# A 64-wide recurrence on Trainium2: its loads cut into 512 KB pieces along the inverse levels, its output products moved between the last three levels

## The chip, the cores and the metric

The kernel runs on one core of one Trainium2 chip. The metric is device time of one execution in microseconds (us); the median over three runs of the kernel before is 5277.31 us (5276.41 to 5279.03). A core has five engines with instruction streams of their own: PE (TensorE, matrix products), DVE (VectorE), ACT (ScalarE), POOL (GpSimd) and SP (SyncE, which here only issues transfers). They meet through semaphores; 16 DMA engines move data between HBM and the on-chip memory.

## What is computed

The reference is a model of two mixing blocks and one block with attention. The change touches one part of the first mixer, a recurrence over 1024 time steps, 8 heads of width 64, run once forward and once backward in time:

```python
def rwkv7_scan(r, w, k, v, a, b):
    def step(state, xs):
        r_t, w_t, k_t, v_t, a_t, b_t = xs
        sa = jnp.einsum('bhvk,bhk->bhv', state, a_t)
        state = state * w_t[:, :, None, :] + sa[..., None] * b_t[:, :, None, :] + v_t[..., None] * k_t[:, :, None, :]
        return state, jnp.einsum('bhvk,bhk->bhv', state, r_t)
    _, y = lax.scan(step, jnp.zeros((bsz, heads, hd, hd), jnp.float32), xs)
...
    wkv = rwkv7_scan(r, w_f, k, v, a_vec, b_vec) + flip_t(
        rwkv7_scan(flip_t(r), flip_t(w_b), flip_t(k), flip_t(v), flip_t(a_vec), flip_t(b_vec)))
```

The kernel does not step through time. It takes chunks of 64 steps: within a chunk the dependence of the steps on each other is a triangular 64 x 64 system, whose inverse is built by doubling, and only the state goes from chunk to chunk.

## The kernel before

The kernel is one long program of stages. The stage of the change is the function `rwkv` (L2041 on), from about 838 us to 1386 us of the profiled execution. Before it an earlier stage writes the decayed factors to HBM (`decayed`, six arrays per direction, and `shared`, of which array 2 holds the values); after it `mixer_outputs` reads the result `yk` and 14 tiles that `rwkv` has prefetched into the buffer `early`.

All of it is done for two directions d = 0 and d = 1, for 16 chunks (RCH) of 64 steps (RH), and for 4 pairs of heads (RPAIRS): a tile [128, 4, 64] holds the 8 heads, two on the partitions (64 each) and four along the free dimension. `by_head` (L2087) issues the products of one term: for each pair h and each half e one 64 x 64 x 64 product in f32, 8 products, which the trace records as 16 matmuls of 64 x 64. That block of 16 records is the unit in which PE's work is counted here. A call with several terms adds them in the same PSUM region.

The loop of PE (L2204 on) has RCH + 1 = 17 turns. Turn i has an inner half, the inverse of chunk i, and an outer half, the state and the outputs of chunk k = i - 1. The order on PE is written out by hand:

- `begin` of both directions (5 blocks each): products of the loaded factors into bank Y, and transposes of values and keys into banks A and D; `gates` (2 blocks each) into bank G.
- level 0 of the inverse: `level_y` (1 block); with it `read_state` (2 blocks) of the chunk before.
- level 1: `level_y`, then `solve` (1 block), then `level_z` (2 blocks).
- level 2: for each direction `level_y` and behind it `outputs` of the chunk before (5 blocks: two state terms, three y terms); then `level_z`.
- levels 3, 4 and 5: `level_y` of both directions, `level_z` of both (2 blocks each, 1 at level 5, where only xt is wanted).

Turn 0 has no outer half, turn 16 no inner one. At each level l >= 1 a chain goes round the engines: Y on PE (needs x of the level before), its copy `ys` on ACT (L2264), Z on PE (the products D and A from ys and xt), then DVE adds D to x (L2331) and A to xt (L2333). Each engine runs its list in order, direction 0 before direction 1.

Further in the outer half: ACT copies `rest` and `u` (L2257, L2270); DVE makes the new state from the first half of bank G (L2340), in its list at level 2 behind the two directions' additions; ACT copies the output y from the second half of bank G to `yk` (L2274), in its list at level 3, and waits for y_out (the products are done) and s_ready (the state is made).

Loads: a group is four chunks (GROUP = 4), 7 arrays of [512, 256] f32 per direction, 512 KB each. Two buffers per direction alternate (`given`; the first lies in `early`). SP issues per group and direction one transfer of 3072 KB (six arrays) and one of 512 KB (L2110, L2111). Groups 0 and 1 are issued at the start, group q >= 2 for direction d when the outputs of all chunks of group q - 2 are done (y_out at 4(q - 1)). PE's `begin` waits for both transfers of its group. When the outputs of chunk 11 are done, SP issues the 14 prefetch transfers of 512 KB for the next stage (L2120). POOL makes the masked blocks `off` of levels 1 to 5 (L2129).

Of the kernel before, what the change touches and what calls it, by code (L numbers as in the profile page):

```python
# [27 lines left out]
P = 128  # L28
# [1506 lines left out]
RPAIRS = 4  # L1535
RCH = T // RH
# [504 lines left out]
def rwkv(nc, tag, decayed, shared, last_decay, consts, early, yk, early_in, prefetch):  # L2041
# [16 lines left out]
    with Stage(nc, tag) as st:  # L2058
# [25 lines left out]
        def pairs(t):  # L2084
            return t.unsqueeze(1).to_broadcast([P, RPAIRS, RH])

        def by_head(pe, out, *terms):  # L2087

            for h in range(RPAIRS):
                for n, (a, b) in enumerate(terms):  # L2090
                    for e in range(2):
                        own = slice(RH * e, RH * e + RH)
                        mm = pe.matmul(out[own, h, :], a[own, h, :], b[own, h, :], start=(n == 0), stop=(n == len(terms) - 1))  # L2093
            return mm

        with nc.Block(no_gpsimd_drain=True) as block:
            @block.sync
            def _(sp):
                for a, b in ((ident[:, :], consts["ident64"]), (masks[:, :, :, :], consts["masks64"]),
                             (strict[:, :, :], consts["strict_half"]), (incl[:, :, :], consts["incl64"])):  # L2100
                    sp.dma_start(a, b).then_inc(const_in, 16)

                def load(q):
                    for d in range(2):
                        if q >= 2:
                            sp.wait_ge(per[d]["y_out"], GROUP * (q - 1))
                        at = GT * (q if d == 0 else RCH // GROUP - 1 - q)
                        split = lambda x: x.rearrange("n (k p) t -> p (n k) t", p=P)[:, :, at:at + GT]
                        to = given[d][q % 2].rearrange("p n k t -> p (n k) t")
                        sp.dma_start(to[:, 0:24, :], split(decayed[d])).then_inc(per[d][f"in{q % 2}"], 16)  # L2110
                        sp.dma_start(to[:, 24:28, :], split(shared[2:3])).then_inc(per[d][f"in{q % 2}"], 16)  # L2111

                load(0)
                load(1)
                for q in range(2, RCH // GROUP):
                    load(q)
                for d in range(2):
                    sp.wait_ge(per[d]["y_out"], RCH - GROUP)
                for slot, source in prefetch:
                    sp.dma_start(early[:, slot, :], source).then_inc(early_in, 16)  # L2120

            @block.gpsimd
# [12 lines left out]
            def _(pe):  # L2135
# [4 lines left out]
                def begin(d, i):  # L2140
                    s = per[d]
                    A, Y, DD, G = banks[d]
                    pe.wait_ge(s[f"in{i // GROUP % 2}"], 32 * (i // GROUP // 2 + 1))
                    pe.wait_ge(s["x_ready"], i * XN)
                    by_head(pe, Y[:, first, :], (piece(d, i, 1), piece(d, i, 0)))
                    by_head(pe, Y[:, second, :], (piece(d, i, 2), piece(d, i, 0))).then_inc(s["aa"], 1)
                    by_head(pe, A[:, first, :], (piece(d, i, 6), one))
                    by_head(pe, A[:, second, :], (piece(d, i, 3), one)).then_inc(s["vb_turned"], 1)
                    by_head(pe, DD[:, first, :], (piece(d, i, 4), one)).then_inc(s["k_turned"], 1)
# [29 lines left out]
                def read_state(d, k):  # L2179
                    s, b, t = per[d], bufs[d], turns[d][k % 2]  # L2180
                    G = banks[d][3]
                    pe.wait_ge(s["s_ready"], k)
                    pe.wait_ge(s["vb_copied"], k + 1)
                    pe.wait_ge(s["g_ready"], min(k + 2, RCH))
                    by_head(pe, G[:, first, :], (piece(d, k, 0), b["s"]), (t["aa"][:, second, :], t["vb"][:, first, :])
                            ).then_inc(s["read"], 1)
# [5 lines left out]
                    pe.wait_ge(s["x_ready"], (k + 1) * XN)  # L2192
                    by_head(pe, G[:, second, :], (t["xt"], b["rest"])).then_inc(s["u_done"], 1)

                def outputs(d, k):
                    s, b, t = per[d], bufs[d], turns[d][k % 2]
                    G, gk = banks[d][3], g[d][k % 2]
                    pe.wait_ge(s["u_copied"], k + 1)
                    by_head(pe, G[:, first, :], (t["vb"][:, second, :], b["u"]), (t["kt"], t["vb"][:, first, :]))
                    by_head(pe, G[:, second, :], (b["s"], piece(d, k, 5)), (b["u"], gk[:, first, :]),  # L2200
                            (t["vb"][:, first, :], gk[:, second, :])).then_inc(s["y_out"], 1)

                for i in range(RCH + 1):
                    inner, outer = i < RCH, i > 0  # L2204
                    for d in range(2):
                        if inner:
                            begin(d, i)
                    for d in range(2):
                        if inner:
                            gates(d, i)  # L2210
                    for d in range(2):
                        if inner:
                            level_y(d, i, 0)
                        if outer:
                            read_state(d, i - 1)
                    for d in range(2):
                        if inner:
                            level_y(d, i, 1)
                    for d in range(2):
                        if outer:  # L2220
                            solve(d, i - 1)
                        if inner:
                            level_z(d, i, 1)
                    for d in range(2):
                        if inner:
                            level_y(d, i, 2)
                        if outer:
                            outputs(d, i - 1)
                    if inner:
                        for d in range(2):  # L2230
                            level_z(d, i, 2)
                        for l in range(3, LV):
                            for d in range(2):
                                level_y(d, i, l)
                            for d in range(2):
                                level_z(d, i, l)

            @block.scalar
            def _(act):
                for i in range(RCH + 1):  # L2240
# [17 lines left out]
                    for l in range(1, LV):  # L2258
# [6 lines left out]
                        for d in range(2):  # L2265
                            s = per[d]
                            if outer and l == 1:
                                act.wait_ge(s["u_done"], k + 1)
                                act.wait_ge(s["y_out"], k)
                                act.activation(bufs[d]["u"][:, :, :], banks[d][3][:, second, :], ACT.Copy).then_inc(s["u_copied"], 1)  # L2270
                            if outer and l == 3:
                                act.wait_ge(s["y_out"], k + 1)
                                act.wait_ge(s["s_ready"], k + 1)
                                act.activation(yk[:, d, :, chunk(d, k) * RH:(chunk(d, k) + 1) * RH], banks[d][3][:, second, :],  # L2274
                                               ACT.Copy).then_inc(s["y_copied"], 1)

            @block.vector
            def _(dve):
# [5 lines left out]
                for i in range(RCH + 1):  # L2284
# [38 lines left out]
                    for l in range(1, LV):  # L2323
# [10 lines left out]
                                                  ALU.add).then_inc(s["x_ready"], 1)  # L2334
                        for d in range(2):
                            s, b = per[d], bufs[d]
                            if outer and l == 2:
                                dve.wait_ge(s["s_decayed"], k + 1)
                                dve.wait_ge(s["y_out"], k + 1)
                                dve.tensor_tensor(b["s"][:, :, :], b["sd"][:, :, :], banks[d][3][:, first, :],  # L2340
# [3366 lines left out]
```

## Time and profile before

| | |
|---|---|
| median of the runs | 5277.31 us |
| profiled execution, its span | 5269.1 us |
| PE busy | 4796.6 us, 91% of the span |
| DVE, ACT, POOL busy | 2724.4, 1100.7, 731.5 us |
| the stage, from its first DMA issue to the last copy of y | 838.3 to 1386.1 us |
| of it PE on the products of Y and Z | banky 107.0, banka 109.0, bankd 87.6 us |

The profile is of one execution; the span runs from the first to the last instruction, and the measured time of a run includes what lies around it. Lines name an engine, a source line and an operation with output and inputs; since `by_head` issues all products, they all stand on L2093 and are told apart by their tiles: `rk_banky<-rk_x,rk_off` is Y, `rk_bankd<-rk_ys,rk_xt` and `rk_banka<-rk_xt,rk_ys` are the two products of Z, `rk_bankg<-...` belongs to gates, state and outputs, and the first products of a turn are `rk_banky<-kept_held` or `rk_banky<-rk_in`, after the two load buffers. PEclk is the mean granted clock of PE, 1.00 being 2.4 GHz. A releaser "issue" means that the engine waited for nothing that the profile shows. Turn i begins at 854.22 (i = 0), 894.21, 924.62, 955.83, 986.41, 1021.56, 1057.14, 1087.54, 1117.95, 1154.08, 1188.18, 1218.70, 1249.11, 1281.99, 1316.25, 1346.87 and 1377.19 us; direction 1 of turn 0 starts at 865.66 us, when its data is there. SP issues the loads of group 2 from 1002.5, of group 3 from 1134.9 and the prefetch from 1268.1 us.

### The profile page before, as it was taken

The numbers are of one execution on the slowest core, as the hardware profiler recorded it, in microseconds if no ns is written. First come the engines' busy times: TensorE is split into PE (matmuls) and PEld (weight loads), VectorE is DVE, ScalarE is ACT, GpSimd is POOL, SyncE is SP. The second block draws the span as 40 slices with busy tenths as digits, with TensorE's granted clock in tenths as the row PEclk, the third lists the DMA queues.
The fourth block names the chain that finished last, engine by engine and source line by source line (L and its number), as shares of the span: only waits on it lengthen the run. The fifth ranks groups of instructions, "written<-read, shape, count | busy, mean of one in ns | idle before, by whom it ended". The sixth has DMA issues, their size and how long they took to land. (4 is left out here: it accounts for less than half of the span.)

```text
span 5269.1 us, 88450 instructions
## 1 busy us (share of the span) xinstructions
PE 4796.6 (91%) x38282; PEld 3690.1 (70%) x38282; DVE 2724.4 (52%) x3644; ACT 1100.7 (21%) x1513; POOL 731.5 (14%) x666
## 2 busy tenths in 40 slices
PE   9996997999889999888849999999988989999999
PEld 7775987999768767544437767766544557788887
DVE  5776543444445788467765594232563325443342
ACT  2443221222313232101102221111221122110010
POOL 0001331111000164000000010012000000241340
PEclk9998998999898999989979899999999999999999
DMA  4444114111121334512222153246212014212113
GB/s 141 147 161 138 47 41 126 60 60 60 44 92 60 111 140 170 199 64 85 98 82 100 57 166 101 75 115 167 46 25 52 5 43 151 76 48 91 70 50 99
DMA packets 223077, 482.78 MB, mean 92 GB/s; under 512 B 34599, under 2 KB 101097, under 8 KB 222181
## 3 DMA queue, kind: packets, MB, share of 16 engines
q1 hardware_dynamic: 177428, 342.80, 20.1%
q0 software_dynamic: 33392, 117.54, 6.5%
q10 hardware_dynamic: 11872, 16.78, 0.9%
q8 instruction: 306, 5.01, 0.4%
q14 instruction: 79, 0.64, 0.0%
HBM read 332.21 MB, written 142.35 MB: 90 GB/s over the span
## 5 line engine op out<-in xcount | busy, mean ns | idle before, releaser
L4966 PE MATMUL tail_product<-tail_x_hi,tail_w_hi 128*128 128x512 f32 x832 | 329.4, 396 | 12.9 <-DVE tail_x_lo L165 10.9
L4966 PE MATMUL tail_product<-tail_x_lo,tail_w_hi 128*128 128x512 f32 x832 | 325.1, 391 | 0.0
L4966 PE MATMUL tail_product<-tail_x_hi,tail_w_lo 128*128 128x512 f32 x832 | 324.4, 390 | 0.0
L3653 PE MATMUL win_product<-kept_hn_hi,win_w_hi 128*128 128x512 f32 x560 | 230.3, 411 | 8.7 <-DVE kept_hn_lo L3807 6.3
L1777 PE MATMUL front_product<-kept_x_hi,front_w_hi 128*128 128x512 f32 x544 | 220.9, 406 | 10.7 <-DVE kept_x_lo L165 10.5
L3653 PE MATMUL win_product<-kept_hn_lo,win_w_hi 128*128 128x512 f32 x560 | 221.0, 395 | 0.0
L3653 PE MATMUL win_product<-kept_hn_hi,win_w_lo 128*128 128x512 f32 x560 | 220.7, 394 | 0.0
L1777 PE MATMUL front_product<-kept_x_hi,front_w_lo 128*128 128x512 f32 x544 | 213.8, 393 | 0.0
L1777 PE MATMUL front_product<-kept_x_lo,front_w_hi 128*128 128x512 f32 x544 | 213.3, 392 | 0.0
L2770 PE MATMUL oproj_product<-kept_mix_hi,oproj_w_hi 128*128 128x512 f32 x512 | 205.3, 401 | 8.6 <-DVE kept_mix_lo L165 8.6
L2770 PE MATMUL oproj_product<-kept_mix_hi,oproj_w_lo 128*128 128x512 f32 x512 | 200.4, 391 | 0.0
L2770 PE MATMUL oproj_product<-kept_mix_lo,oproj_w_hi 128*128 128x512 f32 x512 | 200.2, 391 | 0.0
L4966 PE MATMUL tail_product<-tail_f_hi,tail_w_hi 128*128 128x512 f32 x480 | 189.6, 395 | 0.0
L4966 PEld LDWEIGHTS tail_product<-tail_x_hi,tail_w_hi 128*128 128x128 f32 x832 | 156.8, 188 | 45.5 <-issue 11.5
L4966 PE MATMUL tail_product<-tail_f_hi,tail_w_lo 128*128 128x512 f32 x480 | 186.8, 389 | 0.0
L4966 PE MATMUL tail_product<-tail_f_lo,tail_w_hi 128*128 128x512 f32 x480 | 186.7, 389 | 0.0
L4966 PEld LDWEIGHTS tail_product<-tail_x_hi,tail_w_lo 128*128 128x128 f32 x832 | 156.8, 188 | 33.0
L4966 PEld LDWEIGHTS tail_product<-tail_x_lo,tail_w_hi 128*128 128x128 f32 x832 | 157.0, 189 | 31.0 <-issue 0.2
L3288 PE MATMUL lc_ps<-lc_idft,lc_zz 128*128 128x256 f32 x512 | 120.6, 400 | 61.9 <-DVE lc_zz L3131 59.2
L3288 PEld LDWEIGHTS lc_ps<-lc_idft,lc_zz 128*128 128x128 f32 x512 | 102.7, 202 | 81.6 <-issue 62.4
L2129 POOL TENSOR_TENSOR rk_off<-rk_aa,rk_masks 128x1280 f32<-128x1280 f32 x32 | 99.2, 3115 | 428.7 <-DVE rk_aa L2293 428.7
L2331 DVE TENSOR_TENSOR rk_x<-rk_x,rk_bankd 128x256 f32<-128x256 f32 x128 | 53.9, 421 | 200.4 <-PE rk_banka L2093 200.4
(748 smaller groups left out, 11271.2 us busy)
## 6 DMA issues: line engine op xcount, KB each, us to landing
s_decayed<-front_ring SPq DMA_DIRECT2D x96, 256.0 KB, 3.9
tail_w<-in_w_gu SPq DMA_DIRECT2D x44, 512.0 KB, 3.2
second_raw<-in_w_in SPq DMA_DIRECT2D x35, 512.0 KB, 3.6
front_w<-in_even_w SPq DMA_DIRECT2D x34, 512.0 KB, 3.9
s_pm<-kept_held SPq DMA_DIRECT2D x64, 256.0 KB, 2.0
win_cq_hi_plain<-in_ada_w POOLq DMA_DIRECT2D x16, 1024.0 KB, 5.4
oproj_ring<-in_odd_w POOLq DMA_DIRECT2D x30, 512.0 KB, 3.8
dn_kv<-s_qkv SPq DMA_DIRECT2D x16, 768.0 KB, 6.7
```

The source lines that it names most:

```text
L1777: mm = pe.matmul(pp[:, u_, f, :], p, q, start=(k == 0 and m == 0), stop=(k == 7 and m == 2))
L2129: pool.tensor_tensor(off[d][:, 1:, :, :], turns[d][i % 2]["aa"][:, first, :].unsqueeze(1).to_broadcast([P, LV - 1, RPAIRS, RH]), masks[:, ...
L2331: dve.tensor_tensor(b["x"][:, :, :], b["x"][:, :, :], DD[:, first, :], ALU.add).then_inc(s["x_ready"], 1)
L2770: mm = pe.matmul(pp[:, u, f, :], p, q, start=(k == 0 and m == 0), stop=(k == 7 and m == 2))
L3288: mm = pe.matmul(out[:, 2 * s + r // 2, r % 2 * 256:r % 2 * 256 + 256], zz[:, r, kind, f, ct * P:(ct + 1) * P], tabi[:, kind, f, r, :], st ...
L3653: mm = pe.matmul(pp[:, u, h, :], l, b, start=(k == 0 and m == 0), stop=(k == depth(s) - 1 and m == 2))
L4966: mm = pe.matmul(pp[:, s % 2, h_, :], l, b, start=(k == 0 and m == 0), stop=(k == deep(s) - 1 and m == 2))
```

## The change

It has two parts. First, SP loads every array by itself, 512 KB each: 14 transfers per group. Group 0 is issued at once. For groups 1, 2 and 3 each transfer waits for one more Y of direction 0 (y_done counts six per turn): the first for Y of level 3 in the first turn of the group before, the 14th for 13 Y's later; directions alternate. The wait for the outputs that still read the buffer stays. The 14 prefetch transfers are spaced in the same way from turn 12, level 3. PE's `begin` waits for seven transfers (112) instead of two (32).

Second, `outputs` is divided. `state_terms` (the two terms that make the new state) stays between the Y's of level 2. The three terms of y go, pair by pair of heads, ahead of the Y's of levels 3, 4 and 5: pairs 0 to 2 of direction 0, then pair 3 of direction 0 with pairs 0 and 1 of direction 1, then pairs 2 and 3 of direction 1. DVE's addition that completes the state and ACT's copy of y are put at level 4 for direction 0 and at level 5 for direction 1, both behind that level's work. `read_state` waits in addition for ACT's copy of the y before.

```diff
@@ by_head
-        def by_head(pe, out, *terms):
+        def by_head(pe, out, *terms, heads=range(RPAIRS)):
-            for h in range(RPAIRS):
+            for h in heads:
@@ SP
-                def load(q):
-                    for d in range(2):
-                        if q >= 2:
-                            sp.wait_ge(per[d]["y_out"], GROUP * (q - 1))
...
-                        sp.dma_start(to[:, 0:24, :], split(decayed[d])).then_inc(per[d][f"in{q % 2}"], 16)
-                        sp.dma_start(to[:, 24:28, :], split(shared[2:3])).then_inc(per[d][f"in{q % 2}"], 16)
+                def piece_in(q, d, n):
+                    at = GT * (q if d == 0 else RCH // GROUP - 1 - q)
+                    source = decayed[d][n] if n < 6 else shared[2]
+                    sp.dma_start(given[d][q % 2][:, n, :, :], tiled(source)[:, :, at:at + GT]).then_inc(per[d][f"in{q % 2}"], 16)
+                def paced(first_level, j):
+                    sp.wait_ge(per[0]["y_done"], first_level + j)
+                for d in range(2):
+                    for n in range(7):
+                        piece_in(0, d, n)
+                for q in range(1, RCH // GROUP):
+                    begun = GROUP * (q - 1) * LV
+                    for n in range(7):
+                        for d in range(2):
+                            if q >= 2 and n == 0:
+                                sp.wait_ge(per[d]["y_out"], GROUP * (q - 1))
+                            paced(begun + 4, 2 * n + d)
+                            piece_in(q, d, n)
                 for d in range(2):
                     sp.wait_ge(per[d]["y_out"], RCH - GROUP)
-                for slot, source in prefetch:
+                for j, (slot, source) in enumerate(prefetch):
+                    paced((RCH - GROUP) * LV + 4, j)
@@ PE
+                    pe.wait_ge(s["y_copied"], k)
...
+                def state_terms(d, k):
+                    pe.wait_ge(s["u_copied"], k + 1)
+                    by_head(pe, banks[d][3][:, first, :], (t["vb"][:, second, :], b["u"]), (t["kt"], t["vb"][:, first, :]))
+                def outputs(d, k, heads):
+                    mm = by_head(pe, banks[d][3][:, second, :], (b["s"], piece(d, k, 5)), (b["u"], gk[:, first, :]),
+                                 (t["vb"][:, first, :], gk[:, second, :]), heads=heads)
+                    if heads[-1] == RPAIRS - 1:
+                        mm.then_inc(s["y_out"], 1)
+                FILL = {3: [(0, range(0, 3))], 4: [(0, range(3, 4)), (1, range(0, 2))], 5: [(1, range(2, 4))]}
@@ PE, the loop
-                            outputs(d, i - 1)
+                            state_terms(d, i - 1)
...
-                        for l in range(3, LV):
+                    for l in range(3, LV):
+                        if outer:
+                            for d, heads in FILL[l]:
+                                outputs(d, i - 1, heads)
+                        if inner:
@@ ACT, the copy of y
-                            if outer and l == 3:
+                            if outer and l == 4 + d:
@@ DVE, the new state
-                            if outer and l == 2:
+                            if outer and l == 4 + d:
```

## Rows read from the trace of the kernel before

**Rows 1.** The head of the page.

```profile
span 5269.1 us, 88450 instructions
```

**Rows 2.** Windows by turn: us, then busy us of each engine, PEclk, DMA share, GB/s.

```profile
865.66:894.21 28.55, 23.45 (x625) 21.86 (x625) 10.35 (x26) 4.81 (x12) 3.14 (x1) 0.92 0.73 232
...
986.41:1021.56 35.15, 32.21 (x964) 31.38 (x961) 14.21 (x32) 7.66 (x20) 6.18 (x2) 0.90 0.56 179
1021.56:1057.14 35.58, 31.42 (x965) 30.47 (x961) 13.21 (x32) 7.74 (x20) 6.25 (x2) 0.95 0.12 36
1057.14:1087.54 30.40, 29.63 (x964) 28.82 (x961) 14.23 (x32) 7.66 (x20) 6.19 (x2) 1.00 0.01 4
...
1117.95:1154.08 36.13, 31.92 (x965) 30.64 (x961) 14.16 (x32) 7.67 (x20) 6.18 (x2) 0.95 0.55 176
1154.08:1188.18 34.10, 31.44 (x964) 30.49 (x961) 13.21 (x32) 7.77 (x20) 6.28 (x2) 0.95 0.12 37
...
1249.11:1281.99 32.88, 30.45 (x964) 29.67 (x961) 14.21 (x32) 7.66 (x20) 6.18 (x2) 0.97 0.41 157
1281.99:1316.25 34.26, 31.02 (x964) 29.93 (x962) 13.21 (x32) 7.66 (x20) 6.26 (x2) 0.98 0.19 72
```

**Rows 3.** Timeline of PE in one turn: start us, us, engine, line, tiles, count.

```profile
1061.82 2.06 PE L2093 MATMUL rk_bankg<-rk_in 64*64 64x64 f32 x64
1063.69 0.66 PE L2093 MATMUL rk_banky<-rk_ident,rk_off 64*64 64x64 f32 x16
...
1077.22 0.66 PE L2093 MATMUL rk_banka<-rk_xt,rk_ys 64*64 64x64 f32 x16
1077.89 0.68 PE L2093 MATMUL rk_banky<-rk_x,rk_off 64*64 64x64 f32 x16
1078.82 0.68 PE L2093 MATMUL rk_banky<-rk_x,rk_off 64*64 64x64 f32 x16 [0.25 <-DVE rk_xt L2333]
1079.31 0.66 PE L2093 MATMUL rk_bankd<-rk_ys,rk_xt 64*64 64x64 f32 x16
...
1086.27 1.35 PE L2093 MATMUL rk_banka<-rk_xt,rk_ys 64*64 64x64 f32 x32
```

**Rows 4.** Timeline of DVE in the same turn, level 2.

```profile
1078.59 0.74 DVE L2340 TENSOR_TENSOR rk_s<-rk_sd,rk_bankg 128x256 f32<-128x256 f32 x2
```

**Rows 5.** Timeline of ACT in the same turn, level 3.

```profile
1078.61 0.39 ACT L2264 ACTIVATE rk_ys<-rk_banky 128x256 f32<-128x256 f32 x1 [4.50 <-PE rk_banky L2093]
1079.54 0.38 ACT L2264 ACTIVATE rk_ys<-rk_banky 128x256 f32<-128x256 f32 x1 [0.55 <-PE rk_banky L2093]
1079.82 0.66 ACT L2274 ACTIVATE kept_held<-rk_bankg 128x256 f32<-128x256 f32 x2
```

**Rows 6.** Timeline of all engines in the last turn, where two handovers are bare.

```profile
1379.27 0.38 ACT L2257 ACTIVATE rk_rest<-rk_bankg 128x256 f32<-128x256 f32 x1 [0.55 <-PE rk_bankg L2093]
1379.71 0.55 PEld L2093 LDWEIGHTS rk_bankg<-rk_rest,rk_xt 64*64 64x64 f32 x16 [0.15 <-ACT rk_rest L2257]
...
1382.84 0.42 DVE L2340 TENSOR_TENSOR rk_s<-rk_sd,rk_bankg 128x256 f32<-128x256 f32 x1 [4.34 <-PE rk_bankg L2093]
...
1383.36 0.38 ACT L2274 ACTIVATE kept_held<-rk_bankg 128x256 f32<-128x256 f32 x1 [2.54 <-DVE rk_s L2340]
```

**Rows 7.** Timeline of PE while the loads of group 2 run.

```profile
1011.24 0.48 PE L2093 MATMUL rk_bankd<-rk_ys,rk_xt 64*64 64x64 f32 x5 [2.15 <-issue]
...
1026.36 0.85 PE L2093 MATMUL rk_banka<-rk_ident,rk_in 64*64 64x64 f32 x22 [3.39 <-issue]
```

**Rows 8.** DMA queues in 1002.5 to 1026.5 (two rows), then in 1057.14 to 1087.54.

```profile
q1 hardware_dynamic: 7232, 7.34, 95.3%
q8 instruction: 3, 0.05, 0.9%
...
q8 instruction: 7, 0.11, 1.4%
```

**Rows 9.** Who waited for whom, PE, 865.66 to 894.21: us in total, times, longest.

```profile
PE rk_banka L2093 <- issue: 2.2, 1, 2.2
```

More of the change, by code:

```diff
@@ L2101, in _ @@
                     sp.dma_start(a, b).then_inc(const_in, 16)
-                def load(q):
-                    for d in range(2):
-                        if q >= 2:
-                            sp.wait_ge(per[d]["y_out"], GROUP * (q - 1))
-                        at = GT * (q if d == 0 else RCH // GROUP - 1 - q)
-                        split = lambda x: x.rearrange("n (k p) t -> p (n k) t", p=P)[:, :, at:at + GT]
-                        to = given[d][q % 2].rearrange("p n k t -> p (n k) t")
-                        sp.dma_start(to[:, 0:24, :], split(decayed[d])).then_inc(per[d][f"in{q % 2}"], 16)
-                        sp.dma_start(to[:, 24:28, :], split(shared[2:3])).then_inc(per[d][f"in{q % 2}"], 16)
[L2113 to L2116, printed above, removed]
+                def piece_in(q, d, n):
[15 more added lines that the diff above has]
+                            piece_in(q, d, n)
                 for d in range(2):
                     sp.wait_ge(per[d]["y_out"], RCH - GROUP)
-                for slot, source in prefetch:
+                for j, (slot, source) in enumerate(prefetch):
+                    paced((RCH - GROUP) * LV + 4, j)
                     sp.dma_start(early[:, slot, :], source).then_inc(early_in, 16)
@@ L2142, in begin @@
                     A, Y, DD, G = banks[d]
-                    pe.wait_ge(s[f"in{i // GROUP % 2}"], 32 * (i // GROUP // 2 + 1))
+                    pe.wait_ge(s[f"in{i // GROUP % 2}"], 112 * (i // GROUP // 2 + 1))
                     pe.wait_ge(s["x_ready"], i * XN)
@@ L2193, in solve @@
                     by_head(pe, G[:, second, :], (t["xt"], b["rest"])).then_inc(s["u_done"], 1)
-                def outputs(d, k):
+                def state_terms(d, k):
                     s, b, t = per[d], bufs[d], turns[d][k % 2]
-                    G, gk = banks[d][3], g[d][k % 2]
                     pe.wait_ge(s["u_copied"], k + 1)
-                    by_head(pe, G[:, first, :], (t["vb"][:, second, :], b["u"]), (t["kt"], t["vb"][:, first, :]))
-                    by_head(pe, G[:, second, :], (b["s"], piece(d, k, 5)), (b["u"], gk[:, first, :]),
-                            (t["vb"][:, first, :], gk[:, second, :])).then_inc(s["y_out"], 1)
+                    by_head(pe, banks[d][3][:, first, :], (t["vb"][:, second, :], b["u"]), (t["kt"], t["vb"][:, first, :]))
+                def outputs(d, k, heads):
+                    s, b, t = per[d], bufs[d], turns[d][k % 2]
+                    gk = g[d][k % 2]
+                    mm = by_head(pe, banks[d][3][:, second, :], (b["s"], piece(d, k, 5)), (b["u"], gk[:, first, :]),
[3 more added lines that the diff above has]
+                FILL = {3: [(0, range(0, 3))], 4: [(0, range(3, 4)), (1, range(0, 2))], 5: [(1, range(2, 4))]}
                 for i in range(RCH + 1):
```

## The prediction

> **What bounds the kernel now.** I read the page's span first, then busy time and granted clock by iteration of the stage that the change touches, then the timelines of PE, DVE and ACT inside one iteration, and last the DMA traffic where iterations are long. The profiled execution spans 5269.1 us [rows 1]; the runs shown have a median of 5277.3, 8.2 above it, and I carry that offset along. Only the recurrence changes (from about 838 to 1386 us, 17 turns of a loop). There PE is the engine with work all the time: in an undisturbed turn, 1057.14 to 1087.54, it is busy 29.63 of 30.40 us at full clock, DVE 14.2, ACT 7.7, POOL 6.2 [rows 2]. A turn with products and inverse both is 60 blocks of 16 matmul records (one term for one direction). Four such blocks take 1063.69-1061.82 = 1.87 us, 0.467 each [rows 3], so the work alone is 28.0 us. The other 2.4 us are four holes, at the start of levels 3, 4 and 5 and of the next turn. I call T0 the start of the last block of a level (product A of direction 1). At T0 = 1077.22 the block runs to +0.47; Y of direction 0 starts at +0.67, Y of direction 1 at +1.60, Z of direction 0 at +2.09 [rows 3]. Three blocks are 1.40, so the hole is 0.69. Its end is set by DVE, which adds the last update to x and xt of direction 1 before Y of direction 1 may start. The fourth hole: the 32 records from 1086.27 need 0.93, the next turn starts at 1087.54, 1.27 later: 0.34 [rows 2, 3].
>
> Six turns are longer than 30.40: 35.15, 35.58, 36.13, 34.10, 32.88 and 34.26, together 208.1, which is 25.7 above six undisturbed ones [rows 2]. In all of them DMA moves data, at a mean of 36 to 179 GB/s against 4, and the mean granted clock is 0.90 to 0.98 [rows 2]. Inside, PE stands still for 2.15 and 3.39 us with "issue" as releaser, so no semaphore kept it [rows 7]. Instructions come by DMA too: queue q8 moved 7 packets in the undisturbed 30.4 us, one in 4.3 us (0.11 MB, so 16 KB each), but only 3 in the 24 us in which q1 moved 7.34 MB at 95% of the engines [rows 8]. I read the stalls as instruction blocks that came late behind load packets; each is followed by a stretch at the lower of the two clocks (1.2 instead of 2.4 GHz), which the mean clock shows.
>
> **Part 1: the loads.** Before, a group of four chunks loads 7.34 MB in one burst of some 24 us; after, it is 14 pieces of 512 KB, one behind each Y of direction 0 from level 3 of the first turn of the group before. At q1's 7.34 MB in 24 us, 306 GB/s [rows 8], a piece is under way for 1.7 us, and levels 3 to 5 are 3.5 us apart. In flight time is 14 x 1.7 = 24 us, as before, but spread over 14/6 = 2.3 turns, 69 us. What goes: the 25.7 us of the six turns, and the 2.2 us stall in turn 0, which overlaps the burst for group 1 [rows 9]; 27.9 us. What comes back: about 16 instruction blocks are fetched in 69 us, 24/69 of them, 5.6, beside a piece. Each may wait between nothing and one whole piece, 1.7 us; four spread loads (three groups and the prefetch for the next stage, which is 14 transfers too) bound this from 0 to 4 x 5.6 x 1.7 = 38 us. I take 1 us per load, 4 us, near the lower end: the mean rest of a piece is 0.85, an engine's share is 32 packets, and PE has always some instructions in hand (the undisturbed turns show no stall with "issue" at all although every block is fetched just in time). A stall of under 1 us should not cost clock: DVE-caused holes of that size stand in every undisturbed turn at clock 1.00 [rows 2]. Part 1: 27.9 - 4 = 23.9 us.
>
> The Trainium skill (DMA: Bandwidth & Descriptors, section Queues, rings and completion order) says that a DMA engine goes round its queues packet by packet, and that a packet is at most 64 descriptors. By that rule a fetch waits for one packet whatever the size of the transfer, and cutting the transfers gains nothing; the sum would be Part 2 alone. The stalls of 2.15 and 3.39 us speak of long waits but don't decide between "a fixed number of descriptors" and "all that is queued".
>
> **The first load** is the same 7.34 MB in the same order (direction 0, then 1), in 14 issues instead of 4. The bytes set its length, not the count of issues: cost 0. Pieces of the later groups come in time: the 14th is released 13 Y's after the first, in turn 2 of 4, a turn and a half before its use. The waits that SP adds stand before nothing but SP's own loads. The prefetch is released from turn 12, level 3, until turn 14, 2 turns before the stage ends.
>
> **Part 2: the output products.** Before, all five terms of the outputs stand between Y of level 2 of the two directions. After, the two state terms (2 blocks, 0.93 us) stay there and the three y terms (3 blocks, 1.40 us per direction, 0.35 per head pair) go ahead of levels 3, 4, 5: 3, 3 and 2 pairs, so 1.05, 1.05 and 0.70 us. Level 2 still has cover: Y of direction 1 needs +1.60 from its T0, as above [rows 3], and gets 0.47+0.47+0.93 = 1.87 at least. In levels 3 and 4 the fill moves Y of direction 1 to +0.47+1.05+0.47 = 1.99, beyond 1.60: DVE is hidden. What is late next is ACT: it starts to copy y 0.72 after Y of direction 0 began (1077.89 to 1078.61 [rows 3, 5]), takes 0.38, PE's weight load follows 0.06 later (1379.27+0.38 to 1379.71 [rows 6]) and the matmul about 0.05 behind it: Z can start 1.21 after Y, and PE has 0.93 of work. A hole of 0.28 stays; 0.69-0.28 = 0.41 gained, twice.
>
> Level 5 gains less. The copy of y moves to the same level as the state's add (level 4 for direction 0), and ACT waits there for the add. DVE comes to it 1.37 after T0 (1078.59-1077.22 [rows 3, 4]), takes 0.42, ACT follows 0.10 later (1382.84 to 1383.36 [rows 6]): +1.89. Queued behind it on ACT is y of direction 0, level 5, ready at 0.47+0.70+0.72 = +1.89; the spacing of two copies is 0.28 (1079.54 to 1079.82 [rows 5]), so it starts at +2.17 and Z at +2.66, where PE would be free at +2.10. Hole 0.56, gain 0.13. Direction 1's pair falls into level 5: DVE's add then ends about 0.9 after the next turn begins, its next work comes 1.2 after; covered by 0.3, and if not, that is the price. The added wait of PE, y copied before the state is read, has everything of PE behind it, but that copy ends some 4 us before; cost 0. The fourth hole stays. Sum: 0.41+0.41+0.13 = 0.95 per turn, 15 turns with both halves: 14.2 us. Turn 0 has no products and the last turn nothing but products in the same order: 0. Bounds: from 0 (each fill only moves the hole) to 15 x 3 x 0.69 = 31.
>
> **Sum.** 23.9+14.2 = 38.1 us. The profiled execution would be 5231.0, the median 5277.3-38.1 = 5239.
>
> **Rivals.**
> (a) Fetches wait for a fixed number of packets, so the same stall time is only strewn about: gain 14.2, 5263. For it: the skill's rule above. Against: the bursts queue 448 KB per engine, a piece 32 KB, less than what the measured stalls need.
> (b) The holes move and don't close, the loads gain: 5277.3-23.9 = 5253. For it: the chain Y, ACT, Z, DVE per level is not shortened, only overlapped; against: the numbers above leave PE 1.05 us to fill 0.69.
> (c) Nothing of a fetch's wait shows, and ACT's chain overlaps more than I think: 27.9+28 = 56, 5221.
> (d) Slower: in a burst a late block holds PE back, so only two fetches per load are hit; strewn pieces may hit 5.6 fetches per load, each with a stall of 2.4 and the loss of clock behind it. One such event now costs 25.7/6 = 4.3 us; 4 x 5.6 x 4.3 = 96 us against 27.9+14.2 gained: 5277.3+54 = 5331. It decides from 42/22.4 = 1.9 us per hit on, more than a piece is under way.
> (e) It doesn't act as described (the paced loads land late, or the stalls have another cause and the fill is nothing): 5277.
>
> **Numbers.** Forecast 0.60 (its own range 5230 to 5250); (a) 0.14, (b) 0.11, (c) 0.07, (d) 0.04, (e) 0.04. The range takes in (a), (b) and part of (c): 5226 to 5265. A measurement of this kernel tells some 0.2%, 10.6 us, from no change. Faster 0.90 (the forecast, (b), (c) and most of (a)), same 0.05, slower 0.05.
>
> **What would show it.** Step 1: turns 4 to 7 of the loop within 1 us of each other, clock 1.00 throughout after 871 us, "issue" stalls of PE under 1 us. Step 2: undisturbed turns of 29.4 to 29.6 us; at levels 3 and 4 PE waits for ACT's ys instead of DVE's xt, for 0.2 to 0.3; at level 5 ACT's copy of y stands right ahead of ys. The prediction is wrong if stalls over 1.5 us with "issue" remain (a, d) or if undisturbed turns stay over 30 us (b).

## The result and the profile after

The changed kernel takes 5236.36 us (median of 4 runs, 5233.85 to 5239.42) against 5276.86 for the kernel before (4 runs, 5272.28 to 5279.03): ratio 0.9932, 95% interval 0.992 to 0.9944. A second comparison gave 5246.3 against 5272.4, ratio 0.9947 (0.9926 to 0.9968). The forecast was 5239 in 5226 to 5265.

The profiled execution spans 5232.0 us, 37.1 less than before [rows 1]. The stage itself, from its first DMA issue to its last copy of y, went from 547.8 to 515.8 us, by 32.0; the other 5.1 us lie in stages that the change doesn't touch. In the profiles of this study all that lies outside the stage takes between 4713 and 4738 us without an edit there, so I count the 32.0 and leave the 5.1 to chance. Another execution of the changed kernel has 519.0 us in the stage.

Windows by turn, as in [rows 2]; the first window is the first load, the second turn 0 from direction 1 on (its first product starts at 865.33):

```profile
838.30:854.86 16.56, 0.00 (x0) 0.03 (x1) 0.18 (x1) 0.00 (x0) 0.00 (x0) 0.50 0.97 305
865.10:889.13 24.03, 22.15 (x625) 20.92 (x625) 10.27 (x25) 4.72 (x12) 3.14 (x1) 0.93 0.18 56
889.13:921.17 32.04, 29.78 (x964) 28.80 (x961) 12.99 (x32) 7.40 (x19) 6.27 (x2) 1.00 0.32 103
...
1011.35:1041.15 29.80, 29.07 (x960) 28.45 (x961) 14.23 (x33) 7.68 (x20) 6.18 (x2) 1.00 0.39 122
1041.15:1071.98 30.83, 29.31 (x960) 28.51 (x961) 14.23 (x33) 7.67 (x20) 6.18 (x2) 1.00 0.31 99
1071.98:1101.32 29.34, 28.86 (x961) 28.35 (x961) 14.21 (x33) 7.67 (x20) 6.17 (x2) 1.00 0.02 5
...
1192.54:1223.73 31.19, 29.84 (x961) 28.76 (x961) 13.32 (x33) 7.68 (x20) 6.27 (x2) 1.00 0.02 4
...
1253.19:1285.08 31.89, 29.51 (x960) 28.64 (x961) 13.34 (x33) 7.68 (x20) 6.17 (x2) 1.00 0.38 132
```

An undisturbed turn takes 29.33 us instead of 30.40. The granted clock is 1.00 in every turn after turn 0, where six turns had 0.90 to 0.98. Turns with loads are not clean, though: up to 2.7 us above 29.33, and one without any load traffic (1192.54, 4 GB/s) is 1.9 above it. Such turns stood in the kernel before too (924.62: 31.21 us at 4 GB/s, 0.8 above 30.40).

PE in the undisturbed turn, from the last block of level 2 on, to be laid beside [rows 3] (blocks of the products in between are left out):

```profile
1089.27 0.66 PE L2093 MATMUL rk_banka<-rk_xt,rk_ys 64*64 64x64 f32 x16
1090.79 1.13 PE L2093 MATMUL rk_banky<-rk_x,rk_off 64*64 64x64 f32 x32
1091.92 0.68 PE L2093 MATMUL rk_bankd<-rk_ys,rk_xt 64*64 64x64 f32 x16
...
1097.45 0.63 PE L2093 MATMUL rk_banka<-rk_xt,rk_ys 64*64 64x64 f32 x16
1098.62 1.10 PE L2093 MATMUL rk_banky<-rk_x,rk_off 64*64 64x64 f32 x32
1100.02 1.15 PE L2093 MATMUL rk_banka<-rk_xt,rk_ys 64*64 64x64 f32 x32 [0.30 <-ACT rk_ys L2284]
```

Both Y's now run as one block of 32 records: the wait for DVE between them is gone. Level 3: T0 to Y 1.52, Y to Z 1.13. Level 5: Y to Z 1.40, and here ACT is the releaser. DVE and ACT around that hole:

```profile
1098.80 0.41 DVE L2360 TENSOR_TENSOR rk_s<-rk_sd,rk_bankg 128x256 f32<-128x256 f32 x1
...
1099.31 0.38 ACT L2294 ACTIVATE kept_held<-rk_bankg 128x256 f32<-128x256 f32 x1 [2.89 <-DVE rk_s L2360]
1099.59 0.65 ACT L2284 ACTIVATE rk_ys<-rk_banky 128x256 f32<-128x256 f32 x2
```

ACT was idle for 2.89 us, waited for the new state, copied y, and only then came to ys. Who kept PE waiting from 870 to 1354 us (us in total, times, longest):

```profile
PE rk_banka L2093 <- ACT rk_ys L2284: 4.5, 15, 0.3
PE rk_banky L2093 <- issue: 3.9, 6, 1.5
PE rk_bankd L2093 <- issue: 1.7, 4, 0.9
PE rk_bankg L2093 <- issue: 1.5, 3, 0.8
PE rk_banka L2093 <- issue: 1.0, 2, 0.7
PE rk_banky L2093 <- DVE rk_xt L2353: 1.0, 4, 0.3
```

"issue" sums to 8.1 us, none over 1.5 (18.7 before, up to 3.4); DVE's xt fell from 12.0 to 1.0. Of the 8.1, 7.7 lie in turns 1 to 15; the other 0.4 is in the last turn and is a wait of another kind (shown further down).

The ledger of the stage, in us gained: turns 1 to 15 took 483.0 and take 454.9. Of these 28.1, 15 x (30.40 - 29.33) = 16.0 are the shorter undisturbed turn, and 12.1 are what lay above it (27.0 before, 14.9 after). Turn 0 with its wait for direction 1 went from 40.0 to 34.3: 5.7. The first load took 1.1 longer, the last turn 0.65. Together 32.0. The first load and turn 0 belong together: PE starts direction 1 when its data is there, 27.3 us after the stage's start before and 27.5 after. So the 1.1 us delays direction 0 alone and is won back in the wait for direction 1; from direction 1's start, turn 0 is 4.75 us shorter. In it PE had stalls with "issue" of 2.2, 0.9 and 0.2 us before and none after, and it is busy for 22.15 us instead of 23.45.

### The profile page after: what moved, and what is told of

The parts are those of the page before. It is cut to its first block and busy times, and to the rows that moved or that the text cites. A ratio compares the mean times of both kernels' runs of the same rounds, so it can differ in the third digit from the quotient of the medians.

```text
span 5232.0 us, 88526 instructions
## 1 busy us (share of the span) xinstructions
PE 4770.3 (91%) x38282; PEld 3668.8 (70%) x38282; DVE 2724.5 (52%) x3644; ACT 1101.0 (21%) x1513; POOL 732.9 (14%) x666
## 5 line engine op out<-in xcount | busy, mean ns | idle before, releaser
L4986 PE MATMUL tail_product<-tail_x_hi,tail_w_hi 128*128 128x512 f32 x832 | 329.4, 396 | 11.9 <-DVE tail_x_lo L165 10.8
L3673 PEld LDWEIGHTS win_product<-kept_hn_hi,win_w_hi 128*128 128x128 f32 x560 | 106.4, 190 | 60.7 <-issue 32.1
```

The costliest lines, as they stand in the source:

```text
L3673: mm = pe.matmul(pp[:, u, h, :], l, b, start=(k == 0 and m == 0), stop=(k == depth(s) - 1 and m == 2))
L4986: mm = pe.matmul(pp[:, s % 2, h_, :], l, b, start=(k == 0 and m == 0), stop=(k == deep(s) - 1 and m == 2))
```

## The experiments

One number is used throughout: the loss, turns 1 to 15 together less 15 undisturbed turns (of 30.40 us in the old order of products, 29.33 in the new one). It holds what late instructions cost. The stalls are those of the whole stage from 870 us on, turn 0 included. Stage, loss and stalls are of one profiled execution each.

| kernel | stage us | loss us | PE stalls with "issue" us | median us (before, same chip) |
|---|---|---|---|---|
| before | 547.8 | 27.0 | 18.7 | |
| loads alone | 538.9 | 21.8 | 12.7 | 5267.4 (5274.1) |
| loads alone, again | 538.3 | 20.1 | 10.8 | 5262.9 (5270.2) |
| products alone | 535.0 | 28.9 | 23.8 | 5266.0 (5274.1) |
| changed | 515.8 | 14.9 | 8.1 | 5236.4 (5276.9) |
| changed, again | 519.0 | 17.1 | 11.5 | 5246.3 (5272.4) |
| pieces not paced | 537.3 | 30.8 | 24.7 | 5251.6 (5272.4) |
| pieces in pairs | 524.7 | 22.6 | 16.7 | 5246.2 (5272.4) |
| pieces one Z later | 519.7 | 19.3 | 10.0 | 5247.4 (5272.9) |
| halves | 514.4 | 13.3 | 7.7 | 5238.9 (5272.9) |
| no loads of groups 2 and 3, group 1 at the start | 512.4 | 6.7 | 5.1 | 5237.5 (5272.4) |
| both copies at level 5 | 520.7 | 19.4 | 13.3 | 5243.4 (5274.1) |
| split fill | 516.3 | 26 (from 28.6) | 15.8 | 5238.3 (5274.1) |
| split fill, halves | 507.6 | 17 (from 28.6) | 9.6 | 5233.5 (5272.9) |

**Each part alone.** The kernel before with the SP block and the 112 of the change (e1), and the changed kernel with SP's block of before (e2).

```diff
e1_loads, on the kernel before
-                for q in range(2, RCH // GROUP):
-                    load(q)
+                            paced(begun + 4, 2 * n + d)
+                            piece_in(q, d, n)
...
e2_products, on the changed kernel
-                            paced(begun + 4, 2 * n + d)
-                            piece_in(q, d, n)
+                for q in range(2, RCH // GROUP):
+                    load(q)
```

> Only the loads are changed (14 paced pieces per group); the output products stay as before. Theory A (part 1 is worth what the changed kernel's trace shows, turn 0 and the long turns, 16 us in the stage, and the rest of the gain lies in other stages by chance of the clock): undisturbed turns stay at 30.4 us, no PE stall with issue over 1.8 us, the turns 1 to 15 lose about 10 us to late instructions or less, because the holes at levels 3 to 5 give the fetch slack; median 16 to 20 us below the kernel before. Theory B (part 1 is worth the 24 us of my prediction and only the denser stream of the products takes it back): the turns 1 to 15 lose under 6 us, 22 to 26 us below.

> Only the output products are moved; loads as before, in bursts. Undisturbed turns near 29.33 us as in the changed kernel, six long turns as before, some 4 us above the others each. If parts add up: 16 us below the kernel before (15 turns by 1.07). If the denser instruction stream is late by itself (turns without any load at 30.3 and 31.2 us in the changed kernel suggest it), turns without loads scatter between 29.3 and 31 and the gain is 8 to 12 us.

Loads alone: ratio 0.9987 (0.9977 to 0.9998), stage 8.9 us shorter. Products alone: 0.9989 (0.9977 to 1.000), stage 12.7 shorter; its undisturbed turns are 29.33, as expected. Its long turns look worse, up to 39.15 us:

```profile
1018.46:1057.61 39.15, 32.61 (x960) 31.68 (x961) 13.22 (x33) 7.76 (x20) 6.25 (x2) 0.91 0.44 139
```

But a burst that took two turns before now falls mostly into one, since the outputs that free the buffer come later in the turn: for group 2 the two turns 35.15 and 35.58 of [rows 2] are 9.9 us above two undisturbed ones, here the two turns 29.62 and 39.15 are 10.1 above. So a burst costs about what it did (loss 28.9 against 27.0).

The parts sum to 21.6 us, both together give 32.0 (or 28.8). Loads alone kept the undisturbed 30.40 and lost 21.8 us above it, twice what theory A allowed and far from B's 6; one stall with "issue" reached 2.05 us, over A's 1.8, and the median is 6.7 us lower, not 16 to 20. Because the surplus could have been the chance of one execution, both kernels were run again.

> The changed kernel once more, unchanged, to see how much of the stage's time is chance of one execution. If the stage's 515.8 us repeat within 3 us, the 10 us by which both parts together beat the sum of the parts alone (8.9 and 12.7 against 32.0 in the stage) are real. If it takes 520 to 526 us, the late instruction blocks fall differently from execution to execution and the parts do add up.

> The kernel with the loads alone changed, once more. Its stage took 538.9 us, 8.9 less than before, where the changed kernel's own turns let 16 expect. If that is the chance of one execution, as the 3 us between two executions of the changed kernel are, the stage now takes 532 to 536 us and the parts add up; if it repeats at 537 to 541 us, spread loads help less beside the old order of the products, and the two parts need each other.

519.0 and 538.3: the changed kernel moves by 3 us between executions, the loads alone by 0.6. So the surplus of 7 to 10 us is more than these two move by; the kernel before and the products alone, which the sum needs too, were profiled once. The medians point the same way: 6.7 and 7.3 us for the loads alone, 8.1 for the products alone, 40.5 and 26.1 for both. The whole surplus lies in the loss: paced loads take 5.2 to 6.9 us off it in the old order of the products (27.0 to 21.8 and 20.1), and 11.8 to 14.0 in the new one (28.9 to 17.1 and 14.9). In the second execution of the loads alone a turn with pieces shows full clock, 30.69 us of PE busy instead of 29.63, and 1.7 us more idle time:

```profile
1020.98:1054.15 33.17, 30.69 (x964) 29.29 (x961) 13.31 (x33) 7.67 (x20) 6.27 (x2) 1.00 0.34 103
1087.43:1117.83 30.40, 29.63 (x964) 28.82 (x961) 14.22 (x32) 7.68 (x20) 6.18 (x2) 1.00 0.02 4
```

Why pieces cost more beside the old order of products than beside the new one, these runs don't tell. The clock is not it: from turn 1 on it is 1.00 in both.

**Size or spacing.** Three edits of the pacing, and one that takes the loads away: groups 0 and 1 are loaded at the start, groups 2 and 3 are left out, so that the later chunks work on the first groups' data again, and only the prefetch is still paced. The pairs are for groups 1 to 3, the prefetch stays as it was. `paced_again` waits for direction 1's z_done of the same level. The edits are cut to their main lines.

```diff
e4_unpaced
-                    sp.wait_ge(per[0]["y_done"], first_level + j)
...
e8_pairs
-                            paced(begun + 4, 2 * n + d)
+                            paced(begun + 4, 2 * n)
...
e9_halves
+                            piece_in(q, d, n, (0,))
+                            paced_again(begun + 4, 2 * n + d)
+                            piece_in(q, d, n, (1,))
...
e5_no_loads
-                for q in range(1, RCH // GROUP):
+                for q in range(1, 1):
```

> The changed kernel with the 512 KB pieces but without the pacing: each group's 14 pieces are issued at once when the buffer is free, as one burst. If it is the spacing that helps, the burst behaves as in the kernel before: stalls of 2 to 3 us with issue and a granted clock under 1.00 in six turns, 26 to 30 us lost, stage near 532 us. If it is the size of a transfer (a fetch waits for one transfer at most), stalls stay under 1.7 us and the stage near 516 to 520 us.

> The changed kernel with two pieces (1 MB) released at every second Y instead of one at every Y, groups 1 to 3; the same bytes and the same spread. If a fetch waits for all that is queued, its mean wait doubles while half as many bursts are met: stalls with issue of up to 2.5 to 3 us, granted clock under 1.00 in some turns, 8 to 12 us more than the changed kernel. If a fetch waits for a packet only, no difference.

> The changed kernel with every piece cut in two (256 KB each, the prefetch too): the first half is released by the same Y of direction 0, the second by the end of direction 1's Z of that level (at level 0 both by the Y). If a block of instructions waits for what is queued ahead of it and has some slack, the wait falls from at most 1.7 us to at most 0.9 and nearly disappears: of the 14 to 17 us that turns 1 to 15 lose in the changed kernel 5 or less remain, the stage takes 505 to 508 us, 8 to 12 us less for the whole. If the bytes in flight alone count, however cut, it stays at 516 to 519 us.

> The changed kernel, but the loads of groups 1, 2 and 3 are left out: group 0 and group 1 are both loaded at the start and used again, so chunks 8 to 15 repeat data; the prefetch stays. If the remaining losses of turns 1 to 15 (14.5 us above 29.33 each in the changed kernel) come from pieces in flight, turns 4 to 11 all take 29.33 and the stage gains 8 to 10 us more. If the dense instruction stream is late by itself, turns 4 to 11 scatter up to 31 as now. The extra burst for group 1 runs under turn 0 and will cost 3 to 5 us there.

The same bytes cost 30.8 us in bursts of 7.3 MB, 22.6 in pairs of 1 MB, 14.9 and 17.1 in 512 KB, 13.3 in 256 KB. Without the three groups 6.7 are left, of which 4.3 are the two turns with the prefetch. So it is the spacing: 14 transfers of 512 KB issued at once are as bad as four large ones (30.8 against 28.9 for the products alone, which differs only in how the bursts are cut and ordered). The burst of pieces brings back the lower clock in three turns (0.96, 0.92 and 0.95), where six were expected. The pairs cost 6 to 9 us of the stage, near what was expected, but with stalls of 1.8 us at most instead of 2.5 to 3, and at clock 1.00. Without the loads turns 4 to 11 lose 1.7 us together, 7.1 and 9.3 in the changed kernel: nearly all of that loss is of the pieces. The stage is 3 to 7 us shorter, with the burst in turn 0 that comes back. One turn of each, unpaced, in pairs and without loads:

```profile
1019.76:1057.70 37.94, 31.05 (x961) 30.17 (x961) 14.03 (x33) 7.68 (x20) 6.15 (x2) 0.96 0.54 175
```

```profile
1018.52:1050.67 32.15, 29.37 (x960) 28.59 (x961) 13.92 (x33) 7.67 (x20) 6.17 (x2) 1.00 0.35 112
```

```profile
1014.74:1044.08 29.34, 28.86 (x961) 28.34 (x961) 14.22 (x33) 7.69 (x20) 6.18 (x2) 1.00 0.02 5
```

The longest stall with "issue" is 3.2 us in the unpaced kernel, 1.8 with pairs and 1.2 with halves:

```profile
PE rk_bankg L2093 <- issue: 8.5, 6, 3.2
```

```profile
PE rk_bankg L2093 <- issue: 5.0, 6, 1.8
```

```profile
PE rk_banky L2093 <- issue: 3.3, 4, 1.2
```

(PE's waits in the unpaced kernel, in pairs, in halves.) The longest stall alone is a coarse measure: between kernels with 512 KB pieces it runs from 1.0 (one Z later) to 2.05 us (loads alone), so it tells bursts from pieces, but not pairs from single pieces.

The trace's list of DMA packets shows the cause more directly. In the kernel before, each of the 8 stalls over 0.5 us ends 2.3 to 2.7 us after a 16 KB packet on q8, the instruction queue, has started; in the eleven executions of the table's first eleven lines it is so for all 90 stalls over 0.5 us, with 2.2 to 3.2 us. One such packet comes per 256 recorded instructions of PE (weight loads and matmuls). Without load traffic it starts at the same place of the 256, give or take 30; beside load packets it starts later, by a median of 129 to 166 instructions in the three kernels with bursts, 57 in pairs, 35 to 49 in 512 KB pieces and 29 in halves. An instruction is 15.8 ns of an undisturbed turn (30.40 us for 1921), so that is 2.0 to 2.6, 0.9, 0.6 to 0.8 and 0.5 us. An instruction block does come late, and the later, the more is queued beside it.

The halves missed their expectation: they took 2 to 4 us off, not 10. With two executions of the changed kernel 2.2 apart and one of the halves, even that is not sure; in any case a part of the loss doesn't shrink with the piece. In the kernel without loads the burst for group 1 lies under turn 0 again, and that turn takes 39.95 us, with a clock of 0.78, against 34.3 and 35.4 with 0.85 and 0.83: so 4.6 to 5.7 us of the gain come from turn 0.

```profile
856.49:896.44 39.95, 29.41 (x705) 27.92 (x705) 11.38 (x27) 5.81 (x14) 6.21 (x2) 0.78 0.83 264
```

**The place of a piece.**

```diff
e11_later
                     sp.wait_ge(per[0]["y_done"], first_level + j)
...
+                    sp.wait_ge(per[0]["z_done"], i * (LV - 1) + l)
```

> The changed kernel with each piece released by the end of direction 0's Z of the same level, about 2 us later, the same size and number. If only size and spacing count, the stage stays at 514 to 521 us. If the place of a piece against the fetches of instruction blocks (8 to a turn) decides, the loss of turns 1 to 15 moves by more than 5 us either way.

519.7 us and a loss of 19.3, 2 to 4 more: within what was expected if place counts little.

**ACT's wait at level 5.**

```diff
e3_copies_last, ACT
-                            if outer and l == 4 + d:
+                            if outer and l == 5:
```

> The changed kernel with one edit: ACT copies both y at level 5, behind that level's ys, instead of direction 0 at level 4. If ACT's wait for the new state makes the hole of level 5 (0.47 us against 0.25 at levels 3 and 4), that hole falls to 0.25 and an undisturbed turn from 29.33 to 29.1 us; the whole by 15 x 0.22 = 3.3 us. If something else makes it, the turn stays at 29.33.

PE of an undisturbed turn, level 5:

```profile
1253.25 0.63 PE L2093 MATMUL rk_banka<-rk_xt,rk_ys 64*64 64x64 f32 x16
1254.42 1.11 PE L2093 MATMUL rk_banky<-rk_x,rk_off 64*64 64x64 f32 x32
1255.53 1.15 PE L2093 MATMUL rk_banka<-rk_xt,rk_ys 64*64 64x64 f32 x32
```

Y to Z is 1.11 us instead of 1.40; the row with ACT's 4.5 us is gone from PE's waits. The mechanism is shown; the shortest turn with both halves takes 29.18 us, where 29.1 was expected. The time did not follow: stage 520.7, 2 to 5 us more than the changed kernel, with 13.3 us of "issue" against its 8.1 and 11.5. That the holes served as slack would explain it, but one execution doesn't show it.

**Splitting the fill.** Built on the one before; one pair of levels 3 and 4 goes behind the Y's, to cover ACT's way too. Then the same with the halves.

```diff
e6_split_fill, PE
-                FILL = {3: [(0, range(0, 3))], 4: [(0, range(3, 4)), (1, range(0, 2))], 5: [(1, range(2, 4))]}
+                FILL = {3: [(0, range(0, 2))], 4: [(0, range(3, 4)), (1, range(0, 1))], 5: [(1, range(2, 4))]}
+                LATE = {3: [(0, range(2, 3))], 4: [(1, range(1, 2))], 5: []}
```

> As the one with both copies at level 5, and one pair of products of levels 3 and 4 is taken from ahead of the Y's and put behind them, ahead of the Z's (two pairs before, one after). It covers DVE's way (needs 0.66 us, gets 0.70) and ACT's (needs 0.20, gets 0.35). The holes of levels 3 and 4 vanish: undisturbed turn 28.6 to 28.7 us, 15 x 0.7 = 10 us below the changed kernel, 50 us below the kernel before. Rival: the holes of 0.2 us were slack that the late instruction blocks used, so part of this comes back as stalls with issue, and the gain over the changed kernel is under 5 us.

> The same halves on the kernel with the products split before and behind the Y's. If the late instruction blocks were what took the gain of the split fill back (31 us lost in turns 1 to 15 against an undisturbed turn of 28.3), half of it returns: stage 496 to 504 us, 15 us below the changed kernel. If the dense instruction stream starves by itself, the stage stays at 508 us or more.

The undisturbed turn falls to 28.6 us, as worked out, but alone (stage 516.3, 5238.3 us) nothing comes of it: 15 x 0.75 = 11 us gained in the undisturbed turn, and the loss, counted from 28.6, is 26 us instead of 15 to 17: the rival of its expectation came. With the halves the loss is 17 and the stage takes 507.6 us, the shortest of all, but longer than the 496 to 504 expected and just at the 508 of a stream that starves by itself; the whole takes 5233.5 (5218.8 to 5246.0) against 5272.9, ratio 0.9936 (0.9916 to 0.9957). In the stage that is 8 to 11 us better than the changed kernel; in the whole the runs can't tell it from the changed kernel. A nearly unbroken turn and one with pieces:

```profile
1009.06:1040.78 31.72, 29.20 (x961) 28.59 (x961) 13.84 (x32) 7.78 (x20) 6.17 (x2) 1.00 0.37 114
1100.17:1128.89 28.72, 28.70 (x961) 28.42 (x961) 14.10 (x32) 7.78 (x20) 6.17 (x2) 1.00 0.10 33
```

PE is busy 28.70 of 28.72 us. Its 60 blocks of 0.467 us are 28.0, so about 0.7 us are left that this measure doesn't show as idle.

## Why the prediction was right, and where not

**Part 2, the products** (forecast 14.2 us). Measured 15 x 1.07 - 0.65 = 15.4. Levels 3 and 4: Y at T0 + 1.52 as forecast; Z followed Y by 1.13 where 1.21 was forecast, since ACT's way is a little shorter than the sum of its parts. Level 5: ACT's add-copy-ys order stood exactly as described, Y to Z 1.40 where T0 + 2.66 had asked for 1.49; the copies experiment took it away and with it the hole. The one step of this part that failed is the added wait of PE at the state's read, costed at nothing: in the last turn no `begin` lies ahead of it, and the turn grew from 8.9 to 9.5 us. ACT's copy for direction 1, which it waits for, starts only behind the add of level 5 and ends at 1345.48; PE, which stood for 0.44 us, goes on 0.1 later. The profile calls this wait "issue", but it is the semaphore:

```profile
1344.59 0.41 DVE L2360 TENSOR_TENSOR rk_s<-rk_sd,rk_bankg 128x256 f32<-128x256 f32 x1
...
1345.10 0.38 ACT L2294 ACTIVATE kept_held<-rk_bankg 128x256 f32<-128x256 f32 x1 [1.81 <-DVE rk_s L2360]
1345.58 0.33 PE L2093 MATMUL rk_bankg<-rk_s,rk_in 64*64 64x64 f32 x4 [0.44 <-issue]
```

**Part 1, the loads** (forecast 23.9). Measured 12.1 in turns 1 to 15, 5.7 in turn 0, -1.1 in the first load: 16.7; by the second execution 13.4. The cause was right: with the bursts went the stalls over 1.5 us and the lower clock, and unpaced they come back (30.8 us). Two terms were mis-sized. What comes back was set at 1 us per load, 4 in all; the loss is 14.9 to 17.1, and 6.7 of it is still there when the three groups are gone. I took that a stall is all that a late block costs; but in turns 1 to 15 the stalls with "issue" make up 7.7 of the 14.9, and PE is busy for 439.3 us where 15 undisturbed turns have 432.9, another 6.4 at the same clock and for the same work. I also took it from the undisturbed turns that PE has enough in hand to hide most of the wait of a fetch. It has not, and the holes that the fill closed are not the reason: with all of them kept, the loads alone lose more, 21.8 and 20.1. What sets the slack stays open. On the other side turn 0 was counted with its one stall of 2.2 us and gave 4.4 to 4.8 from direction 1's start on: the stalls of 0.9 and 0.2 us and 1.3 us of PE's busy time were left out. "Cost 0" for the first load can stand: direction 0's data came 1.1 us later, direction 1's did not, and the products alone, with the old first load, needed 16.8 us for direction 0 as well.

The prediction said that a stretch at the lower clock follows each stall. It does for the two of [rows 7], not for all: in the three kernels with bursts it is so for 13 of 22 stalls of 1.8 us or more, and in the kernels with paced loads, whose longest stalls from turn 1 on are 1.0 to 2.05 us, for none.

**The signs.** Clock 1.00 after turn 0 came, undisturbed turns under 30 us came (29.33, slightly under the 29.4 to 29.6 named). Two signs of step 1 did not: turns 4 to 7 lie 1.5 us apart (29.33 to 30.83), not within 1, and stalls reach 1.5 us, not under 1, just at the bound from which the prediction called itself wrong.

**The sum.** 38.1 forecast; in the stage 32.0 and 28.8. The medians' differences are 40.5 and 26.1, with intervals from 17 to 42 us together. That the first lies so close to the forecast is luck: 5 to 8 us of it come from outside the stage. The prediction was right in its time, 6 to 9 us too high in its mechanism.

**Rivals.** (a), the same stall time strewn about, falls: "issue" went from 18.7 to 8.1 and 11.5 us, and with the same number of transfers the loss is 30.8 in a burst and 15 to 17 spaced. The Trainium skill (DMA: Bandwidth & Descriptors, Queues, rings and completion order) says that a DMA engine drains a whole packet, of at most 64 descriptors, from one queue before it turns to the next. If each of the 1 KB packets that the profile counts is one descriptor, 64 of them are 3.4 us at an engine's share of the 306 GB/s of [rows 8]; this is an estimate from the page's ceiling. The longest stall in a burst, 3.39 us, is of that size. The 9 to 17 descriptors that the page calls typical would be 0.5 to 0.9 us by the same estimate, less than the 2.0 to 2.6 us by which a fetch in a burst starts late here in the median. A piece of 512 KB brings an engine 32 of them, 1.7 us by the same estimate. So the prediction's reading, that by this rule the size of a transfer can't matter, was too short: below such a packet it can. The 3.2 us with unpaced pieces would need a packet over more than one transfer, and no run here shows where a packet ends. Whether a fetch waits for such a packet or for all that is queued stays open. (b) falls: the holes closed, 29.33. (c) and (d) did not come. What none of them held is that the two parts give more together than alone, where they give 8.9 and 12.7.

## What to carry to other kernels

Where an engine issues small instructions without a break, as PE does here with one in 15.8 ns, its own instruction stream is a load like any other, and a burst of data transfers starves it: look for stalls with "issue" beside high DMA traffic, and space the transfers by progress of the work, in small pieces. Filling holes of such an engine pays only as far as its instructions come in time; here fill and pacing tried one by one gave 12.7 and 8.9 us, both 32.0 and 28.8, so try them together before you drop either. When two engines hand over in order (here DVE's add, ACT's copy), put the copy a step behind the add, not into the same step ahead of critical work. That closed the hole, though here the whole got no shorter by it.

## What the runs showed of the hardware

- PE fetches its instructions in 16 KB packets on queue q8, one per 256 instructions. Beside load packets they start late: a median of 2.0 to 2.6 us in bursts of 7.3 MB, 0.9 with 1 MB released at a time, 0.6 to 0.8 with 512 KB, 0.5 with 256 KB. PE then stalls with "issue" and goes on 2.2 to 3.2 us after the start of the packet (90 stalls).
- The longest stalls are 2.8 to 3.4 us in bursts, 1.8 with 1 MB, 1.0 to 2.05 with 512 KB and 1.2 with 256 KB.
- Late blocks cost more than stalls: PE is busy for 439.3 us instead of 432.9 in 15 turns at full clock. Turns without load traffic can be long too (31.19 us at 4 GB/s against 29.33).
- Transfers cut small but issued at once gain nothing (loss 30.8 against 27.0 and 28.9 for large ones).
- The granted clock falls to its lower level behind 13 of 22 stalls of 1.8 us or more in the kernels with bursts, and from turn 1 on behind none of those of 1.5 to 2.05 us in the kernels with paced loads.
- Stages that no edit touched took from 4713 to 4738 us together in 14 profiled executions; a difference of 10 us in the whole is read from the stage, not from the total.
